# Two transformer blocks on one core: an aligned shared buffer, a fifth leading block, a later gate, two last tiles on GpSimd

## The reference

```python
# first block: chunked attention, gated convolution, squared-relu MLP
h = rms_norm(x, norm1_g); q, k, v, bg, cg, xc = split(h @ w_in)
merged = g_attn * (y_attn @ w_attn_proj) + g_conv * (y_conv @ w_conv_proj)
x = x + merged @ w_out
x = x + square(relu(rms_norm(x, norm2_g) @ w_up)) @ w_down
# second block, layers 0 and 1; mem is 256 positions of memory
for layer in (0, 1):
    u = rmsnorm(h, norm_g[layer, 0]); mem_kv = mem_n @ w_mem_kv[layer]
    if layer == 0: y = mixer_window_attn(u, mem_kv, ...)   # window attention + cross-attention to mem
    else:          y = mixer_hgrn2(u, mem_kv, ...)         # gated linear attention, 8 heads + cross-attention
    h = h + rmsnorm(y, norm_g[layer, 1])
    f = (gelu(dwconv(gate)) * up) @ ffn_w_out[layer]       # gate, up = split(rmsnorm(h, ...) @ ffn_w_in[layer])
    h = h + rmsnorm(f, norm_g[layer, 3])
# a head of mixer_hgrn2: q = silu(..), forget gate f = lb + (1 - lb) * sigmoid(..), key = 1 - f,
# log f summed within chunks of 16, both directions; output * silu(g)
```

## Time and profile before

| what | value |
|---|---|
| time, median of 3 runs | 2439.69 us (2438.66 to 2440.32) |
| the profiled execution's own time | 2437.65 us |
| its span, first to last instruction | 2435.9 us |
| TensorE busy | 98% |
| VectorE, ScalarE, GpSimd busy | 51%, 27%, 60% |
| mean granted TensorE clock | 0.993 |
| DMA | 214.49 MB, mean 88 GB/s |
| longest single waits of TensorE | start 9.3 us; then 2.5 us and less |

### The profile page before, as it was taken

One profiled execution on the slowest core, in us unless ns is written; L12 is line 12 of the kernel. 1 busy time (PEld: TensorE's weight loads), 2 busy tenths in 40 slices (PEclk: granted clock), 3 DMA queues, 4 the chain that ended last, 5 costly groups with the idle time before them and its releaser, 6 DMA issues.

```text
span 2435.9 us, 32669 instructions
## 1 busy us (share of the span) xinstructions
PE 2378.2 (98%) x12126; PEld 1961.1 (81%) x12126; DVE 1231.5 (51%) x2000; ACT 659.7 (27%) x1331; POOL 1466.4 (60%) x1461
## 2 busy tenths in 40 slices
PE   8999999999999999999999999999999999999997
PEld 6877778887888888787788888887888877888885
DVE  4335654334302315777348553044888885755402
ACT  3233321002201213455221110025567643111100
POOL 8654546667666677654458777662344455877761
PEclk9999999999999999999999999999999999999998
DMA  4222222222232322221122222221222212222221
GB/s 169 93 96 87 79 78 97 99 98 88 96 98 98 124 95 87 78 79 62 61 87 96 96 95 95 95 87 53 70 70 70 71 60 78 96 95 97 101 97 52
DMA packets 59762, 214.49 MB, mean 88 GB/s; under 512 B 6624, under 2 KB 6752, under 8 KB 59488
## 3 DMA queue, kind: packets, MB, share of 16 engines
q1 hardware_dynamic: 56880, 206.55, 25.1%
q10 hardware_dynamic: 2736, 5.96, 0.7%
HBM read 210.38 MB, written 2.10 MB: 87 GB/s over the span
## 4 chain that ended last, share of the span: by engine, by line
PE 92%; DVE 5%; ACT 2%; issue 1%; DMA 0%; POOL 0%; DVEq 0%; ACTq 0%; POOLq 0%
PE acc L556 25%; PE acc L558 25%; PE acc L557 24%; PE ps_o L727 2%; PE ps_s L699 2%; PE ps_t L713 2%; PE acc L768 1%; PE acc L770 1%; PE acc L769 1%; PE ps_s L1016 1%; DVE ps_s L1594 1%; PE ps_o L1075 0%; PE ps_s L770 0%; PE ps_s L768 0%; PE ps_s L769 0%
## 5 line engine op out<-in xcount | busy, mean ns | idle before, releaser
L513 POOL CAST w_hi<-w_raw 128x512 fp32r<-128x512 f32 x688 | 439.5, 667 | 709.8 <-DMA w_raw<-stream 709.8
L556 PE MATMUL acc<-h_hi,w_hi 128*128 128x512 f32 (+1 forms) x1844 | 726.0, 394 | 5.5 <-DVE h_lo L1560 2.6
L558 PE MATMUL acc<-h_hi,w_lo 128*128 128x512 f32 (+1 forms) x1844 | 706.7, 383 | 0.0
L557 PE MATMUL acc<-h_lo,w_hi 128*128 128x512 f32 (+1 forms) x1844 | 705.4, 383 | 0.0
L515 POOL TENSOR_TENSOR w_lo<-w_raw,w_hi 128x512 fp32r<-128x512 f32 x384 | 521.6, 1358 | 213.3 <-ACT w_hi L1469 213.3
L517 POOL TENSOR_TENSOR w_lo<-w_raw,w_hi 128x512 fp32r<-128x512 f32 x384 | 534.4, 1392 | 0.0
L556 PEld LDWEIGHTS acc<-h_hi,w_hi 128*128 128x128 f32 x1844 | 348.1, 189 | 73.6 <-DVE h_lo L1560 4.4
L558 PEld LDWEIGHTS acc<-h_hi,w_lo 128*128 128x128 f32 x1844 | 347.2, 188 | 69.8
L557 PEld LDWEIGHTS acc<-h_lo,w_hi 128*128 128x128 f32 x1844 | 348.0, 189 | 65.4 <-issue 1.9
L1616 DVE COPY y_all<-acc 128x512 f32<-128x512 f32 x31 | 21.4, 692 | 269.9 <-PE acc L558 238.5
L556 PE MATMUL acc<-hid_hi,w_hi 128*128 128x512 f32 x352 | 138.9, 395 | 0.0
(11 more groups left out here) (344 smaller groups left out, 3691.0 us busy)
## 6 DMA issues: line engine op xcount, KB each, us to landing
w_raw<-stream SPq DMA_DIRECT2D x384, 512.0 KB, 3.2
toeplitz<-ext_in ACTq DMA_DIRECT2D x16, 256.0 KB, 3.7
out<-x_res SPq DMA_DIRECT2D x4, 512.0 KB, 2.6
x_res<-x_in SPq DMA_DIRECT2D x3, 512.0 KB, 6.8
mem<-mem_in ACTq DMA_DIRECT2D x1, 1024.0 KB, 7.7
consts<-consts_in SPq DMA_DIRECT2D x1, 656.0 KB, 9.3
x_res<-x_in SPq DMA_DIRECT2D x2, 256.0 KB, 5.0
rope<-rope_in ACTq DMA_DIRECT2D x1, 512.0 KB, 9.2
```

Source lines behind the costliest of these rows:

```text
L513: nc.gpsimd.tensor_copy(hi[:, half], raw[:, half]).then_inc(hi_made, 1)
L556: nc.tensor.matmul(ps, hi, x_hi[:, k, 0:cols], start=(k == 0), stop=False)
L557: nc.tensor.matmul(ps, hi, x_lo[:, k, 0:cols], start=False, stop=False)
L558: mm = nc.tensor.matmul(ps, lo, x_hi[:, k, 0:cols], start=False, stop=(k == st.kt - 1))
```

## The change

Four edits, independent of each other.

1. **Placement.** `zero`, `k_g8`, `eps_d`, `eps_q`, `eps_v` and `root_warm` become six neighbouring columns of one buffer `columns`, and `at` is rounded up to 512 bytes instead of 64. The arena now begins 114,176 bytes behind `base`, 64 bytes lower, at a multiple of 512; every tile in it, and `rope`, `ffn_tmp` and `rstd_in`, moves with it. `h_hi`, `h_lo` and the weights stay.
2. **Fifth leading block.** `a_out` gets `WIDE` bank 4 (`ps_s0`) for its block 4. Four of the block's twelve tiles run before `out_lead(11)`, eight behind it; later blocks take the `acc` banks one turn earlier, here and in the stages that follow.
3. **First head's gates.** In layer 1's cross-attention the sigmoids stand behind unit 11, the forget keys behind 12, the logarithms behind 14, and the silu behind the whole attention.
4. **Two last tiles.** GpSimd does tiles 5 and 6 of the last `add_norm`: y by gain ahead of time, then y by root and the sum with x once ScalarE has copied the spread root to `rstd_in`; TensorE spreads it a second time, into `ps_t`, for that. VectorE does the six others. The stores are 0-1, 2-3, 4, 5-6, 7.

```diff
-WIDE = {"ffn_in0": (4, 5, 6), "ffn_in1": (4, 5, 6), "b_in": (6, 5), "b_out": (4,)}
+WIDE = {"ffn_in0": (4, 5, 6), "ffn_in1": (4, 5, 6), "a_out": (4,), "b_in": (6, 5), "b_out": (4,)}
...
-        at = (at + 63) // 64 * 64
+        for i, name in enumerate(["zero", "k_g8", "eps_d", "eps_q", "eps_v", "root_warm"]):
+            small[name] = small["columns"][:, i:i + 1]
+        at = (at + 511) // 512 * 512
...
+            for first, end in ((0, 2), (2, 4), (4, 5)):
+                sp.wait_ge(x_ready, 3 * DT + end)
+                store(first, end)
+            sp.wait_ge(x_pool, len(POOL_TILES))
+            store(5, 7)
+            sp.wait_ge(x_ready, 3 * DT + DT - len(POOL_TILES))
+            store(7, 8)
...
+            for i in POOL_TILES:
+                y, g = y_all[:, i, :], param("norm_g", 56 + i)
+                pool.wait_ge(y_sq, 3 * DT + i + 1)
+                nc.gpsimd.tensor_tensor(y, y, g.to_broadcast([P, T]), ALU.mult).then_inc(pool_own, 1)
+            pool.wait_ge(rstd_copied, 1)
+            for i in POOL_TILES:
+                y = y_all[:, i, :]
+                pool.wait_ge(pool_own, 2 + (i - POOL_TILES[0]))
+                nc.gpsimd.tensor_tensor(y, y, rstd_in[:], ALU.mult).then_inc(pool_own, 1)
+                pool.wait_ge(pool_own, 3 + (i - POOL_TILES[0]))
+                nc.gpsimd.tensor_tensor(x_res[:, i, :], x_res[:, i, :], y, ALU.add).then_inc(x_pool, 1)
...
                 if then is not None:
                     turning(then, 9)
+                else:
+                    for b in range(BLOCKS):
+                        mm = nc.tensor.matmul(ps_t[:, b * P:(b + 1) * P], rstd[:, b:b + 1].to_broadcast([P, P]), const("ident"),
+                                              start=True, stop=True)
+                    mm.then_inc(y_rstd_spare, 1)
...
             st = out_st
+            pe.wait_ge(s_used, n["unit"])
+            lead_tiles = BANKS * st.kt
+            block_tiles(st, lead_tiles, lead_tiles + 4, o_hi2, o_lo2)
             for k in range(len(A_OUT_TURNS), st.kt):
                 out_lead(k)
-            mixer_out(st, o_hi2, stages["ffn_in0"])
+            block_tiles(st, lead_tiles + 4, lead_tiles + st.kt, o_hi2, o_lo2)
+            mixer_out(st, o_hi2, stages["ffn_in0"], BANKS + 1)
...
-            attention(units_x[1], probs2, probs2_t, {5: lambda: head_gates(0), 9: lambda: head_sigmoids(0),
-                                                     10: lambda: head_forget(0), 12: lambda: head_logs(0)})
+            attention(units_x[1], probs2, probs2_t, {len(units_x[1]) - 5: lambda: head_sigmoids(0), len(units_x[1]) - 4: lambda: head_forget(0),
+                                                     len(units_x[1]) - 2: lambda: head_logs(0)})
+            head_gates(0)
...
             post_norm(stages["ffn_out1"], sq=ffn_tmp)
+            act.wait_ge(y_rstd_spare, 1)
+            nc.scalar.activation(rstd_in[:], ps_t[:], ACT.Copy).then_inc(rstd_copied, 1)
...
                 scaled_y(0)
-                for i in range(DT):
+                tiles = [i for i in range(DT) if next_gain is not None or i not in POOL_TILES]
+                for i, after in zip(tiles, tiles[1:] + [None]):
                     step.wait()
                     step(nc.vector.tensor_tensor(x_res[:, i, :], ps_s[i % 2][:], x_res[:, i, :], ALU.add), x_ready)
-                    if i < DT - 1:
-                        scaled_y(i + 1)
+                    if after is not None:
+                        scaled_y(after)
```

More of the change, by code:

```diff
@@ L213, in build @@
         small = {}
-        for name, n in [("zero", 1), ("k_g8", 1), ("half_gate_b", 16), ("lower", 16), ("one_less", 16), ("less_one", 16), ("eps_d", 1), ("eps_q", 1),
-                        ("eps_v", 1), ("neg_sink", 16), ("neg_max", P_BUFS), ("row_sum", P_BUFS), ("sink_exp", P_BUFS), ("inv_sum", P_BUFS),
+        for name, n in [("half_gate_b", 16), ("lower", 16), ("one_less", 16), ("less_one", 16), ("neg_sink", 16), ("neg_max", P_BUFS), ("row_sum", P_BUFS), ("sink_exp", P_BUFS), ("inv_sum", P_BUFS),
                         ("rms_tok", BLOCKS), ("rstd_tok", BLOCKS), ("eps_tok", BLOCKS),
@@ L218, in build @@
                         ("block_f", BLOCKS), ("block_b", BLOCKS),
-                        ("lb_exp", 32), ("root_warm", 1), ("rstd_mem", MEM)]:
+                        ("lb_exp", 32), ("columns", 6), ("rstd_mem", MEM)]:
             small[name] = sb(name, [n], at)
             at += -(-4 * n // 32) * 32
-        at = (at + 63) // 64 * 64
+        for i, name in enumerate(["zero", "k_g8", "eps_d", "eps_q", "eps_v", "root_warm"]):
+            small[name] = small["columns"][:, i:i + 1]
+        at = (at + 511) // 512 * 512
         rope = sb("rope", [2, T], at)
@@ L381, in build @@
         o_copied = sem("o_copied")
+        y_rstd_spare = sem("y_rstd_spare")
+        rstd_copied = sem("rstd_copied")
+        pool_own = sem("pool_own")
+        x_pool = sem("x_pool")
         eps_made = sem("eps_made")
@@ L470, in token_made @@
             return (tok_made, (BLOCKS - 1) * g + b + 1) if b < BLOCKS - 1 else (slot_done, st.first_slot + st.slots)
+        POOL_TILES = (5, 6)
         ACT_SLOTS = range(stages["b_in"].first_slot + 11, stages["b_out"].first_slot + 7)
@@ L491, in _, with store @@
                         .then_inc(loaded[s], 16)
[L493 to L496, removed]
+            def store(first, end):
+                sp.dma_start(out[:, first:end, :], x_res[:, first:end, :]).then_inc(stored, 16)
+            for first, end in ((0, 2), (2, 4), (4, 5)):
[5 more added lines that the diff above has]
+            store(7, 8)
+            sp.wait_ge(stored, 16 * 5)
         @block.gpsimd
@@ L568, in bank_free @@
                     pe.wait_ge(stages["v1"].free, c + 1)
-                elif c == BANKS and st.name != "b_out":
+                elif c == BANKS and st.name not in ("a_out", "b_out"):
                     pe.wait_ge(s_used, n["unit"])
```

## The result

| | before | after |
|---|---|---|
| median of the runs | 2439.18 us (2438.5 to 2440.32, 4 runs) | 2420.87 us (2420.43 to 2422.1, 4 runs) |
| ratio | | 0.9925, 95% interval 0.9908 to 0.9942 |
| the profiled execution: own time, span | 2437.65, 2435.9 us | 2420.69, 2418.9 us |
| mean granted clock | 0.993 | 0.996 |

A forecast was written before the change was run, and what follows sets the result against it. TensorE, busy 98% of the span, was taken as the bound. Terms 8.0 + 2.65 + 4.2 + 3.05 = 17.9 us, off 2439.69, gave 2421.8, rounded to 2422 us; range 2416 to 2431.

The forecast's parts named there:

- Placement, 8.0 forecast: Stretches on arena tiles: remainder 0 instead of 64 makes triples cheaper, 8.0 us gained, bounds 0 and 9.
- the 6.6 ns: TensorE's triples with both moving operands in the arena: each is 6.6 ns dearer than on `h_hi`/`h_lo`.
- the rival with distance or region: Arena triples: distance or region, not remainder, makes the 6.6 ns; placement gains 0, time 2429.8 us; chance 0.16.
- The argument by which I preferred the remainder: Leading `b_out` triples, 0.70 us each, and up blocks losing 0.07: mismatched remainders cost, a change of place alone doesn't.
- equal remainders cost: Arena triples: sharing the weights' remainder makes them dear, 14 to 20 us lost against 9.9 gained; chance 0.03.
- Fifth leading block, 2.65: `a_out`: four triples run earlier, so the waits for `o_lo` and the `acc0` copy go; 2.65 us gained, bounds 1.9 and 2.7.
- Gates, 4.2: Layer 1's cross-attention: four table loads replace six, last `weigh` 4.75 us earlier; 4.2 us taken, bounds 1.5 and 5.5.
- The half-speed stretch that I took 0.55 off for: Cross-attention, behind the second stall of 2.3 us: TensorE's clock may fall, and half of 3.4 us goes.
- a margin for head 0: First head after the cross-attention: of 3.9 us in hand on VectorE's product about 1.9 go, so the delay is covered.
- Two last tiles, 3.05: Last `add_norm`: GpSimd takes two tiles, last store lands at 2432.4 against 2435.5; 3.05 us gained, bounds 0.5 and 3.6.
- Both costs that I had bounded: Kernel's end: second spread 1.05 us at full, 2.05 at half clock; GpSimd operations 1.29 us median, 2.21 at most.
- The sign by counts: Windows of hidden-value stretches: 442 products in 100 us where 438 stood; with the first rival the count stays.

The follow-up runs named there:

- p_64: The changed kernel with the arena 64 bytes higher, so its remainder to 512 bytes is 64 again: 2426.68 us, ratio 0.9949 to the kernel before.

## Why the prediction was right

**Placement, 8.0 forecast.** 7.9 alone, 7.9 by the starts. The counts and the 6.6 ns held (6.6 measured over 128 triples), the up blocks gave 0.07 each. The remainder was the cause, as taken with 8 in 10; the rival with distance or region fell with p_64. With it fell the rule of the Trainium skill, "SBUF — State Buffer", section "Who interferes with whom", that the PE never waits on anyone and reads weights and moving operand through independent ports, as far as the time follows from it. Three places give three rates, 680.0, 686.6 and 700.0 ns, at one granted clock of 1.00, and only the difference from the weights' place tells them apart.

The argument by which I preferred the remainder was weaker than its result: I had no view that varied it, and the earlier trace rows didn't show what I read in them. The same leading triples after the change, where both halves have the weights' remainder:

```profile
1958.08 0.40 PE L580 MATMUL acc<-o_hi_heads,w_hi 128*128 128x512 f32 x1
...
1958.77 0.40 PE L580 MATMUL acc<-o_hi_heads,w_hi 128*128 128x512 f32 x1
...
1959.46 0.39 PE L580 MATMUL acc<-o_hi_heads,w_hi 128*128 128x512 f32 x1
```

They take 691 and 697 ns, against 695 and 701 before: nearly all of their excess over 680 comes behind the small products ahead of them, whatever the remainder. The starts from 1958.08 on are 236, 224, 231, 236, 228, 233 and 230 ns apart, and behind the arena tile in the up block before they are 235, 225, 230, 236, 229, 232 and 231: the same series. So coming to 128x512 products from small ones costs up to some ten dear starts, and one arena tile with a remainder of 64 sets off the like. Mixed halves do cost in a running stream: seven such triples in a row behind the leading ones (from 2023.80 us) averaged 696 ns before and take 680 after, so 16 ns each, of which the forecast had 20. The rival "equal remainders cost" fell too: equal is the fastest seen.

**Fifth leading block, 2.65.** 3.1 by the starts. The waits were read right. Part of the extra 0.4 is what a restart costs that no wait row shows. Timeline of TensorE before, behind the two waits:

```profile
1203.09 0.50 PE L556 MATMUL acc<-o_hi,w_hi 128*128 128x512 f32 x1 [1.87 <-DVE o_lo L1538]
...
1206.91 0.50 PE L556 MATMUL acc<-o_hi,w_hi 128*128 128x512 f32 x1 [0.78 <-DVE y_all L1616]
```

Each took 0.50 us where the others take 0.39, and the next start came 339 ns behind it in place of 227: 0.2 us for the two. The rest isn't accounted for.

**Gates, 4.2.** 5.0. The chain of ScalarE was right to 0.3 us: last scores to last weighing is 1680.96 - 1666.90 = 14.06 us, worked out 14.3. The stalls were 1.09 + 1.12 where I had one of 1.6, and 2.06 where I had 2.3. The half-speed stretch that I took 0.55 off for didn't come in this execution; it came in six of the ten with the later gates, so that it stayed away here is luck. The forecast of a margin for head 0 held: the last key product ends at 1709.14 and TensorE comes for it at 1711.02 without a wait, 1.9 us in hand where 2.0 was forecast.

**Two last tiles, 3.05.** 3.2. Both costs that I had bounded were at their lower end: the second spread ran at full clock, 1.06, and GpSimd's four operations took 1.27 each. VectorE's last operation ended 9.06 us after its first began, with 9.1 forecast.

**What the forecast left out.** Head 7's 2.1 us the other way and 0.7 at the start, against terms that were each a little larger. The sum of the four terms was 19.2 by the starts and 17.9 in the forecast; the span shows 17.0 and the medians 18.3. So part of the agreement to 1 us is luck: the clock's place in one execution is worth 2 us, and I had treated the execution's waits as fixed. The sign by counts was a coarse one as well: 442 products in 100 us were forecast, and a window of 70 us, 1510 to 1580, counts 311 after and 308 before, so one product more or less is a third of what is to be read. My rates by counts, 226.1 and 228.3 ns, were both about 0.6 ns too low (226.7 and 228.9 by the starts); their difference was right.

## What to carry to other kernels

Where TensorE streams without a wait, compare its start-to-start rate between operands that lie in different buffers: a difference of 1% at one granted clock is worth a look at the addresses' distance from the weights, since 64 bytes cost 1% here and 128 bytes 3%. Before a wait is taken away, count the table loads of the engine that it waits for and put functions that need other tables behind the last use of the present one. And where TensorE stalls by a few us in all, as around the last weighings and in head 7 here, the clock fell in some executions and not in others: compare several traces before a loss of 2 us is put down to an edit.

## What the runs showed of the hardware

- A 128x512 product on TensorE takes 226.7 ns start to start, as a mean over a triple, when the moving operand's distance from the weights is 0 or 256 bytes over a multiple of 512, 228.9 at 64 and 233.3 at 128 (triples of 680.0, 686.6 and 700.0 ns). Moving everything by 64 bytes or to true multiples of 512 changes nothing (680.0). Why is open.
- Behind small products, some ten products of 128x512 start 224 to 237 ns apart before the pitch settles at 226.7 (changed kernel, from 1958.08 us); one tile of another remainder in the stream does the same (before, from 618.42 us, 73 ns in all).
- The same stall of 2.05 us cost TensorE half its clock in one execution and nothing in another. Two programs that are alike up to 2400 us, the kernel before and the one with the two last tiles on GpSimd, differed by 2 us in head 7, with a wait of 3.66 us and half speed behind it in place of 2.39.
